# A hybrid encoder trunk on one core: another way to start the first unit of weights, and another way to sum the final norm

## The reference, cut to what matters

```python
def rmsnorm(x, g):
    y = xf * lax.rsqrt(jnp.mean(xf * xf, axis=-1, keepdims=True) + RMS_EPS)
    return y * g
def swiglu(x, wg, wu, wd):
    return (jax.nn.silu(x @ wg) * (x @ wu)) @ wd
for l in range(DEPTH):                       # DEPTH = 2
    x = x + 0.5 * swiglu(rmsnorm(x, ffn1_norm[l]), ...)   # 1024 -> 2816 -> 1024
    x = x + (even_mixer if l % 2 == 0 else odd_mixer)(rmsnorm(x, mix_norm[l]), ...)
    x = x + 0.5 * swiglu(rmsnorm(x, ffn2_norm[l]), ...)
return rmsnorm(x, final_norm)
```

## Time and profile before

| what | value |
|---|---|
| time, median of 3 runs (lowest to highest) | 2061.62 us (2060.53 to 2062.73) |
| span of the profiled execution, first to last instruction | 2062.5 us; no other time of that execution is given |
| PE busy | 1952.7 us, 95% of the span |
| DVE / ACT / POOL busy | 997.9 / 706.1 / 334.4 us |
| mean granted TensorE clock | 0.982 of full speed |
| moved by DMA | 176.66 MB, mean 86 GB/s |
| chain that ended last, by engine | PE 83%, DVE 8%, ACT 4%, POOL 2%, issue 2% |

### The profile page before, as it was taken

The page is one execution under the profiler, slowest core; times in us unless marked ns, Lnnn a source line. Parts: engine busy times, 40 slices in busy tenths (PEclk is TensorE's granted clock), DMA queues, the critical chain, the costliest instruction groups (busy, mean ns, idle before and its releaser), DMA issues.

```text
span 2062.5 us, 23191 instructions
## 1 busy us (share of the span) xinstructions
PE 1952.7 (95%) x8888; PEld 1592.7 (77%) x8888; DVE 997.9 (48%) x1058; ACT 706.1 (34%) x932; POOL 334.4 (16%) x274
## 2 busy tenths in 40 slices
PE   6999999997989999999999999999948999999997
PEld 4888888785868888888878888887726778888885
DVE  6334421668778533342163343216988753433223
ACT  4222221436346422221142222214746542222212
POOL 2111100213113211110021111002345221111001
PEclk9999999998989999999999999999979999999998
DMA  4222222221211222222222222222210022222221
GB/s 148 99 102 100 83 102 102 96 78 37 82 42 42 92 92 102 102 88 95 102 82 102 102 93 90 102 102 90 82 41 21 22 82 102 94 89 102 102 102 41
DMA packets 36211, 176.66 MB, mean 86 GB/s; under 512 B 12752, under 2 KB 13136, under 8 KB 15552
## 3 DMA queue, kind: packets, MB, share of 16 engines
q1 hardware_dynamic: 33696, 172.55, 24.1%
q10 hardware_dynamic: 2304, 2.98, 0.4%
q0 software_dynamic: 160, 0.43, 0.1%
HBM read 173.85 MB, written 2.10 MB: 85 GB/s over the span
## 4 chain that ended last, share of the span: by engine, by line
PE 83%; DVE 8%; ACT 4%; POOL 2%; issue 2%; ACTq 0%; DMA 0%; POOLq 0%; DVEq 0%
PE ps L264 27%; PE ps L266 27%; PE ps L265 27%; POOL acc L333 2%; DVE xgl L299 1%; DVE eD L1180 1%; ACT eD L1135 1%; DVE small L1164 1%; DVE wl L234 1%; ACT wh L230 1%; DVE small L679 1%; DVE th L1755 1%; ACT eA L687 0%; PE ps L862 0%; DVE x L289 0%
## 5 line engine op out<-in xcount | busy, mean ns | idle before, releaser
L264 PE MATMUL ps<-xgh,wh 128*128 128x512 f32 x1792 | 709.9, 396 | 27.7 <-DVE xgl L299 25.4
L265 PE MATMUL ps<-xgl,wh 128*128 128x512 f32 x1792 | 698.8, 390 | 0.0
L266 PE MATMUL ps<-xgh,wl 128*128 128x512 f32 x1792 | 698.8, 390 | 0.0
L234 DVE TENSOR_TENSOR wl<-raw,wh 128x2048 fp32r<-128x2048 f32 (+1 forms) x157 | 360.3, 2295 | 541.1 <-ACT wh L230 541.0
L230 ACT ACTIVATE wh<-raw 128x2048 fp32r<-128x2048 f32 (+1 forms) x157 | 297.9, 1897 | 384.1 <-PE ps L266 382.8
L264 PEld LDWEIGHTS ps<-xgh,wh 128*128 128x128 f32 x1792 | 336.9, 188 | 110.9 <-DVE xgl L299 19.2
L265 PEld LDWEIGHTS ps<-xgl,wh 128*128 128x128 f32 x1792 | 337.0, 188 | 71.0 <-issue 3.4
L266 PEld LDWEIGHTS ps<-xgh,wl 128*128 128x128 f32 x1792 | 336.8, 188 | 71.1
L264 PE MATMUL ps<-ah,wh 128*128 (+1 forms) x704 | 273.9, 389 | 0.0
L265 PE MATMUL ps<-al,wh 128*128 (+1 forms) x704 | 273.9, 389 | 0.0
L266 PE MATMUL ps<-ah,wl 128*128 (+1 forms) x704 | 273.9, 389 | 0.0
(11 more groups left out here) (243 smaller groups left out, 1573.9 us busy)
## 6 DMA issues: line engine op xcount, KB each, us to landing
raw<-in_units SPq DMA_DIRECT2D x161, 1024.0 KB, 4.7
x<-in_xT ACTq DMA_DIRECT2D x8, 256.0 KB, 6.0
outT<-x SPq DMA_DIRECT2D x8, 256.0 KB, 2.1
relb<-in_rpb SPq DMA_DIRECT2D x64, 24.0 KB, 2.1
cosA<-in_rope_a ACTq DMA_DIRECT2D x1, 256.0 KB, 2.7
sinA<-in_rope_a ACTq DMA_DIRECT2D x1, 256.0 KB, 2.9
cosD<-in_rope_d POOLq DMA_DIRECT2D x1, 192.0 KB, 3.0
sinD<-in_rope_d POOLq DMA_DIRECT2D x1, 192.0 KB, 2.7
```

The lines of the kernel that those rows point to most:

```text
L234: nc.vector.tensor_tensor(wl[:, c % 2, 0:n], raw[:, c % 2, 0:n], wh[:, c % 2, 0:n].bitcast(F32), ALU.subtract).then_inc(w_lo, 1)
L264: nc.tensor.matmul(dst, lh, rh, start=first, stop=False)
L265: nc.tensor.matmul(dst, lh, rl, start=False, stop=False)
L266: return nc.tensor.matmul(dst, ll, rh, start=False, stop=last)
```

## The change

- **Start.** SP now issues all of it: unit 0 in four quarters of 512 columns (two blocks of x each need one quarter), each followed by the two blocks of x that it meets (one transfer of 512 KB), and then unit 1. ACT issues only the gains. POOL issues the three constants. ACT and DVE split a quarter of unit 0, then two blocks of x, four times (`first_act`, `first_dve`); then they split unit 1. PE runs both halves of unit 0 side by side, block of x after block of x (`first_blocks_pe`), and then the matmul of the norm's sum.
- **First norm.** The squares of x are taken after the split of unit 1 (`first_squares_act`).
- **Setup.** The small operations stand in the first pair, after the split of the next pair's first unit.
- **Final norm.** POOL does not add. PE multiplies each squared block, 128 columns at a time as the stationary operand, by one column of `ones`, and so gathers the sum as four columns in one bank (`last_sums_pe`: 8 blocks x 4 matmuls of one column). Root and reciprocal are of 128 x 4. DVE writes them on the diagonals of four 128 x 128 squares, and one matmul with `ones` spreads them over the partitions; DVE scales x with the result read from PSUM (`last_dve`). The squares go round three buffers.

```diff
+        def first_act(act):
+            for q in range(4):
+                if q < 3:
+                    act.wait_ge(unit0_in[q], 16)
+                else:
+                    act.wait_ge(raw_in[0], 16)
+                ins = nc.scalar.activation(wh[:, 0, quarter(q)], raw[:, 0, quarter(q)], ACT.Copy)
+                ins.then_inc(unit0_hi, 1) if q < 3 else ins.then_inc(w_hi, 1)
+                if q == 0:
+                    act.wait_ge(gain_in, 16)
+                act.wait_ge(x_in[q], 16)
+                for b in (2 * q, 2 * q + 1):
+                    nc.scalar.activation(xgh[:, b, :], x[:, b, :], ACT.Copy, scale=gain[:, b:b + 1]).then_inc(xg_hi, 1)
...
+        def first_blocks_pe(pe):
+            for k in range(KD):
+                if k % 2 == 0 and k < 6:
+                    pe.wait_ge(unit0_lo, k // 2 + 1)
+                if k == 6:
+                    pe.wait_ge(w_lo, 1)
+                pe.wait_ge(xg_lo, k + 1)
+                for m in range(2):
...
+        def last_sums_pe(pe):
+            for b in range(KD):
+                pe.wait_ge(sq_done, 8 * 6 + b + 1)
+                for t in range(TT):
+                    mm = nc.tensor.matmul(ps[:, 0, t:t + 1], last_square(b)[:, t * P:(t + 1) * P], ones[:, 0:1],
+                                          start=b == 0 and t == 0, stop=b == KD - 1 and t == TT - 1,
+                                          skip_group_check=True)
+                mm.then_inc(sq_sum if b < KD - 1 else ssum_done, 1)
+            pe.wait_ge(last_diag, 1)
+            nc.tensor.matmul(ps[:, 1, :], ones[:, :], sqt[:, :, :].rearrange("p s n -> p (s n)")[:, 0:SEQ],
+                             start=True, stop=True).then_inc(last_rows, 1)
+        def last_square(b):
+            return acc[:, :] if b % 3 == 2 else sqt[:, b % 3, :]
+        def last_squares_act(act):
+            nc.scalar.activation(col(C_STD + 4), col(C_EPS), ACT.Sqrt)
+            for b in range(KD):
+                act.wait_ge(x_new, 8 * 5 + b + 1)
+                if b >= 3:
+                    act.wait_ge(sq_sum, 7 * 6 + b - 2)
...
+        def last_dve(dve):
+            dve.wait_ge(std_done, 7)
+            nc.vector.reciprocal(col(C_RN, 4), col(C_STD, 4)).then_inc(rstd, 1)
...
+            dve.wait_ge(last_rows, 1)
+            for b in range(KD):
+                nc.vector.scalar_tensor_tensor(x[:, b, :], x[:, b, :], gain[:, 6 * KD + b:6 * KD + b + 1],
+                                               ps[:, 1, :], ALU.mult, ALU.mult).then_inc(out_done, 1)
...
+            if first and n == 0:
+                first_blocks_pe(pe)
+                norm_pe(pe, 0, 4)
...
         def ffn_dve(dve, f, B, n, last):
             def pair(p, at_start):
-                split_lo(dve, B + 1, p)
+                if not (at_start and n == 0):
+                    split_lo(dve, B + 1, p)
...
                 split_lo(dve, B + 2, p)
+                if at_start and n == 0:
+                    dve.wait_ge(const_in, 48)
+                    setup_dve(dve)
...
+            for q in range(4):
+                sp.dma_start(raw[:, 0, quarter(q)], units[0:P, quarter(q)]).then_inc(
+                    unit0_in[q] if q < 3 else raw_in[0], 16)
+                sp.dma_start(x[:, 2 * q:2 * q + 2, :],
+                             xT[2 * q * P:2 * (q + 1) * P, :].rearrange("(b p) s -> p b s", p=P)).then_inc(x_in[q], 16)
+            sp.dma_start(raw[:, 1, :], units[P:2 * P, :]).then_inc(raw_in[1], 16)
...
         def _(act):
             act.dma_start(gain[:, :], gains).then_inc(gain_in, 16)
...
-            split_hi(act, 0)
-            finish_act(act, 0)
+            first_act(act)
+            split_hi(act, 1)
+            first_squares_act(act)
             act.wait_ge(const_in, 48)
```

More of the change, by code:

```diff
@@ L189, in vec @@
             return cvec[:, c:c + n]
-        x_in = [sem(f"x_in{b}") for b in range(KD)]
+        x_in = [sem(f"x_in{q}") for q in range(4)]
         gain_in = sem("gain_in")
@@ L219, in build_trunk @@
         setup = sem("setup")
+        unit0_in = [sem(f"unit0_in{q}") for q in range(3)]
+        unit0_hi = sem("unit0_hi")
+        unit0_lo = sem("unit0_lo")
+        last_diag = sem("last_diag")
+        last_rows = sem("last_rows")
         even_in = sem("even_in")
@@ new lines, in first_squares_act, with first_dve @@
+        def first_squares_act(act):
+            for b in range(KD):
+                if b >= 3:
+                    act.wait_ge(sq_sum, b - 2)
+                dst = acc[:, :] if b == 0 else sqt[:, b % 2, :]
+                nc.scalar.activation(dst, x[:, b, :], ACT.Square).then_inc(sq_done, 1)
+        def first_dve(dve):
+            for q in range(4):
+                if q < 3:
+                    dve.wait_ge(unit0_hi, q + 1)
+                else:
+                    dve.wait_ge(w_hi, 1)
+                ins = nc.vector.tensor_tensor(wl[:, 0, quarter(q)], raw[:, 0, quarter(q)],
+                                              wh[:, 0, quarter(q)].bitcast(F32), ALU.subtract)
+                ins.then_inc(unit0_lo, 1) if q < 3 else ins.then_inc(w_lo, 1)
+                for b in (2 * q, 2 * q + 1):
+                    lo_x(dve, 0, b)
@@ new lines, in first_blocks_pe @@
+        def first_blocks_pe(pe):
[6 more added lines that the diff above has]
+                for m in range(2):
+                    o = k * 256 + m * P
+                    mm = three(ps[:, m, :], wh[:, 0, o:o + P], wl[:, 0, o:o + P],
+                               xgh[:, k, :], xgl[:, k, :], k == 0, k == KD - 1)
+                    if k == KD - 1:
+                        mm.then_inc(w_half, 1)
@@ new lines, in last_square @@
+        def last_square(b):
[4 more added lines that the diff above has]
+                act.wait_ge(x_new, 8 * 5 + b + 1)
+                if b >= 3:
+                    act.wait_ge(sq_sum, 7 * 6 + b - 2)
+                if b == 0:
+                    act.wait_ge(rstd, 6)
+                nc.scalar.activation(last_square(b), x[:, b, :], ACT.Square).then_inc(sq_done, 1)
+            act.wait_ge(ssum_done, 7)
+            nc.scalar.activation(col(C_STD, 4), ps[:, 0, 0:4], ACT.Sqrt, bias=col(C_EPS),
+                                 scale=1.0 / D).then_inc(std_done, 1)
@@ new lines, in last_dve @@
+        def last_dve(dve):
+            dve.wait_ge(std_done, 7)
+            nc.vector.reciprocal(col(C_RN, 4), col(C_STD, 4)).then_inc(rstd, 1)
+            dve.wait_ge(rstd, 7)
+            nc.vector.tensor_tensor(sqt[:, 0, :].rearrange("p (t e) -> p t e", t=TT),
+                                    ident[:, :].rearrange("p (o e) -> p o e", o=1).broadcast_to([P, TT, P]),
+                                    col(C_RN, 4).rearrange("p (t o) -> p t o", o=1).broadcast_to([P, TT, P]),
+                                    ALU.mult).then_inc(last_diag, 1)
+            dve.wait_ge(last_rows, 1)
+            for b in range(KD):
+                nc.vector.scalar_tensor_tensor(x[:, b, :], x[:, b, :], gain[:, 6 * KD + b:6 * KD + b + 1],
+                                               ps[:, 1, :], ALU.mult, ALU.mult).then_inc(out_done, 1)
@@ L305, in finish_act @@
                     split_hi(act, split)
[L306 to L309, removed]
+                act.wait_ge(x_new, 8 * (n - 1) + b + 1)
                 if n < 6 and b < held:
@@ L314, in finish_act @@
                                          scale=gain[:, n * KD + b:n * KD + b + 1]).then_inc(xg_hi, 1)
-                if b == 0 and n:
+                if b == 0:
                     act.wait_ge(ssum_done, n)
-                if b == 1 and n:
+                if b == 1:
                     act.wait_ge(sq_sum, 7 * n)
@@ L356, in ffn_up_pe @@
             c0, c1 = B, B + 1
-            pe.wait_ge(w_lo, 2 * p + c0 + 1)
+            if not (first and n == 0):
+                pe.wait_ge(w_lo, 2 * p + c0 + 1)
             if not first:
                 pe.wait_ge(tg_done, 2 * p + 22 * f)
-            for m in range(2):
+            if first and n == 0:
+                first_blocks_pe(pe)
+                norm_pe(pe, 0, 4)
+            for m in () if first and n == 0 else range(2):
                 block_T(pe, ps[:, m, :], c0, m, wait_x=8 * n if first and m == 0 else None).then_inc(w_half, 1)
@@ L442, in ffn_act @@
                 split_hi(act, c + PAIRS)
-            finish_act(act, n + 1)
+            if last:
+                last_squares_act(act)
+            else:
+                finish_act(act, n + 1)
         def ffn_dve(dve, f, B, n, last):
             def pair(p, at_start):
-                split_lo(dve, B + 1, p)
+                if not (at_start and n == 0):
+                    split_lo(dve, B + 1, p)
                 if at_start:
@@ L1891, in _ @@
             nc.gpsimd.memset(ones[:, :], 1.0).then_inc(ones_set, 1)
+            pool.dma_start(small[:, :], consts).then_inc(const_in, 16)
+            pool.dma_start(cvec[:, :], colvec).then_inc(const_in, 16)
+            pool.dma_start(ident[:, :], ident_d).then_inc(const_in, 16)
```

(9 more changed lines are left out.)

10 lines of the change are left out of this document (6 added, 4 removed).

## The result

| | before | changed |
|---|---|---|
| median of 12 runs (lowest to highest) | 2061.3 us (2059.5 to 2067.7) | 2067.0 us (2064.6 to 2072.1) |
| ratio, 95% interval | 1 | 1.0024 [1.0014, 1.0034] |
| span of the profiled execution | 2062.5 us | 2068.0 us |

The changed kernel is slower by 0.24%, 4.9 us by the ratio (2.9 to 7.0), 5.7 by the medians. The forecast was 2064.5 with a range of 2059.3 to 2067.0, and the time (2067.0 by the median, 2066.5 by the ratio) lies at that range's upper end and above the forecast's own range (2063.3 to 2065.8). In the profiled execution the clock fell early, as in the second rival; over all runs and traces it is the start that the forecast had wrong, as shown further down.

A forecast was written before the change was run, and what follows sets the result against it. PE's passes were taken to bound the kernel, so only time before PE is steadily fed and after its last product could move: 2061.6 - 1.0 (start) + 3.9 (end) = 2064.5 us, range 2059.3 to 2067.

The forecast's parts named there:

- the second rival: End: the clock falls early, at 2049.3, in the sums of blocks 3 and 4; end costs 5.9, 2066.5 us; chance 0.13.
- PE's early start is given back: Start: PE finishes unit 0 at about 20.5, then idles until about 28 before the matmul of the norm's sum.
- The size of that step: Start: the third pair of units begins at 64.9 instead of 65.86, a gain of 1.0 us.
- the landing of unit 1: Start: unit 1, last of 4.2 MB in one queue, lands at 14.2 us, bounds 13.4 and 15.5.
- One queue is late: Rival, start: unit 1 lands at 15.5, making everything behind it 1.3 us later, 2065.8 us; chance 0.08.
- The mark of 65.86: Start: when the third pair begins before the change, in us; moving it moves the kernel's end one for one.
- POOL's adds beside DVE: First norm: adds run from 17.3 to 28.2, overlapping DVE's split; if the first add were blocked, the sum ends at 28.3.
- Table loads and constants on POOL: Pairs and start: two more ACT table loads a turn, 1.28 us each, hide in slack; constants are wanted late; cost zero.
- The end at full clock: Final norm: 64 short instructions take 7.3 us and scaling begins at 2055.8 instead of 2054.51, costing 1.3 us.
- The bound of 0.055: End: lowest spacing in us of one-column matmul instructions, if a load of weights overlaps the next.
- The clock's fall: End: the clock falls at 2051.3 during the sums, adding 2.6 us, so the end costs 3.9 us.
- early-fall rival: End: the clock falls already at 2049.3 in the sums, so the end costs 5.9, 2066.5 us; chance 0.13.

The follow-up runs named there:

- pe_late: The changed kernel, but PE waits for all eight low parts of x before its first pass: 2065.1 us, ratio 1.0025 to the kernel before.
- start_only: The changed kernel with the old end put back (POOL's adds, wide root and reciprocal): 2063.0 us, ratio 1.0006 to the kernel before.
- end_wide: The changed kernel, but each summing matmul at the end streams 128 columns of ones instead of one: 2064.4 us, ratio 1.0011 to the kernel before.
- squares_early: The changed kernel, but ACT takes the first three squares of x ahead of its split of unit 1: 2064.8 us, ratio 1.0013 to the kernel before.
- setup_late: The changed kernel with the setup moved to the second half of the first SwiGLU part, without the loop's table loads: 2066.2 us, ratio 1.0023.
- end_wide_only: The old start with the changed end, each summing matmul streaming 128 columns of ones instead of one: one profiled run, 2067.9 us.
- end_only: The kernel before with only the changed end put in: 2065.4 us, ratio 1.0019 to the kernel before.

## Why the prediction came out as it did

- **That PE's early start is given back: right, shown.** The forecast had PE's passes of unit 0 done at about 20.5 and idle to 28.2; they were done at 20.2 and PE idle to 28.85. `pe_late` shows that 8 us of PE's start are worth nothing. In the four traces with the changed order of the first pair and the sum's matmul at half clock (changed kernel, `start_only`, `end_wide`, `squares_early`) the third pair lies 37.0 us behind the sum's matmul, wherever that begins.
- **The size of that step: 1.0 gained forecast, about 1.0 lost.** The term that was mis-sized is the landing of unit 1 (14.2 forecast). ACT stood waiting for that transfer and began its split at 14.97, 15.39, 15.40, 15.78 and 16.04 in the five traces in which it comes first: 15.5 in the mean, which is the condition of the rival *One queue is late*. In the changed kernel's trace, the earliest of them, POOL's start (18.01, forecast 17.3) and the sum's matmul (28.85, forecast 28.2) are later by nearly as much as the split. Another 0.3 is the pair at half clock: 2.08, forecast 1.8. The later steps came as forecast: 11.6 to the end of unit 2's split (42.54), then the new wait for unit 3 (1.08, forecast 1.2). The mark of 65.86 that the forecast started from was itself 0.4 later than the mean of the old start, and the 0.24 us outside the span stood in no term.
- **POOL's adds beside DVE.** The forecast weighed the rule of the Trainium skill's page SBUF — State Buffer, "Who interferes with whom", by which POOL's first add would be blocked until DVE's split of unit 1 ends. POOL's first add began at 18.01, within DVE's 16.92 to 19.21, and the seven took 10.78 where they take 9.83 without DVE beside them. So the overlap cost 0.95 us, nearly what was left of the split (1.2). The trace agrees with the rule: the longest add, 2.35 us, is the first, and it ended 1.15 us behind the split; the others took 1.26.

```profile
L428 POOL TENSOR_TENSOR acc<-acc,sqt x7: 1259/1262/2345, 18.0 to 27.5; 128x512 f32<-128x512 f32 x7
```

- **Table loads and constants on POOL: nothing, as forecast.** The row that answers to the earlier trace rows has ACT busy for 48.4 us instead of 33.1, and PE for all 114 as before. `setup_late` without the loads is no faster than its wait explains.

```profile
66.00:180.00 114.00, 114.00 (x505) 94.48 (x504) 45.16 (x44) 48.37 (x44) 12.93 (x10) 1.00 0.26 92
```

- **The end at full clock: +1.3 forecast, +1.1 shown** by `end_wide` and `end_wide_only`. The forecast had 0.114 us for a one-column instruction with 128-row weights from one with one row; 16 took 1.84 us. The bound of 0.055 appears in no run.
- **The clock's fall: the mechanism right, its time 2 us off in the profiled execution.** The forecast put it at 2051.3, where it fell before; it fell at 2049.2 (early-fall rival: 2049.3). The sums then took 10.7 us instead of 9.4, and the tail grew by 5.5, where the forecast had 3.9 and the rival 5.9. It is no fixed time: of the five traces with the one-column sums behind the product, three have tails of 12.4 to 12.9 (falls 5.0 to 5.6 after the product's last pass began), as forecast, and two 14.3 and 14.4 (falls 3.4 and 3.5 after it). Their mean is 13.3. The old end has two tails as well, 8.85 and 9.84, 9.3 in the mean, so the changed end costs 4.0, and the time of `end_only` is 4.0 above before: in the mean of these few traces and of the runs, the forecast's 3.9 for the end came.
- **The Trainium skill on the clock.** TensorE: Matmul & The Clock Gate, "What's actually happening", ties the clock to how busy PE has been. The changed start agrees: PE stood idle for 8.62 us, and its next matmul ran at half clock. But the record of PE is no measure of it: in both forms PE was recorded busy without a gap and loaded the same weights; with one column in each matmul the clock fell from 2.4 to 1.2 GHz in five traces of five, with 128 it stayed in two of two.
- **The sum.** The forecast's change was 2.9 us (1.0 gained at the start, 3.9 lost at the end), the measured one 4.9 by the ratio: about 1.0 lost at the start and 4.0 at the end. The miss is the start. That the early-fall rival's 2066.5 lies near the measured time is luck: it had the end 1.9 too dear and the start 2.0 too cheap.

## What to carry to other kernels

Before an engine is fed earlier, find the next row of its queue that waits for another chain: the start of the first block was no bound here, the sum of the first norm was, and a kernel with that chain shortened as well was 7.8 us faster. Here a sum moved from an idle engine to the bounding one, behind that engine's last work, took 9 to 11 us of it in the traces, although its matmuls have one column. In these traces a tail of one-column matmuls ran partly at full and partly at half clock, though PE was never idle: price such a tail at half clock, or make its matmuls wide.

## What the runs showed of the hardware

- One-column matmuls with a full load of weights each: 0.11 us apart at full clock and 0.21 at half (16 instructions in 1.84 and 3.55 us). Widening them to 128 columns costs 0.1 us in 16 (1.95 us) and kept the clock at 1.00 in both traces, for over 7 us.
- The clock also falls at different places in the mixers from run to run, which moves the whole end. With the same old start, the product's last pass began at 2041.8 in `end_only` and 2048.1 in `end_wide_only`; both are the same code up to there. (The two ran on different chips; the kernel before has a median of 2061.4 on each.) The third pair begins at 65.40 and 65.36, so the difference comes later. From 460 to 640 the granted clock was 0.95 in the first and 0.91 in the second, and 0.04 of 180 us is 7 us:

```profile
460.00:640.00 180.00, 157.08 (x857) 126.05 (x855) 142.79 (x204) 92.52 (x198) 45.34 (x44) 0.95 0.18 57
```

```profile
460.00:640.00 180.00, 157.69 (x815) 126.70 (x813) 136.91 (x192) 86.76 (x184) 43.97 (x41) 0.91 0.18 57
```

  This is one source of the 4 to 9 us between the fastest and the slowest run of each kernel, and why a difference of 1 us is read here from distances within a trace.
